# Two transformer blocks on one core: the first modulation weights in feature-block groups, and layer 1's first four projection pairs in plain fp32

## The reference, cut to what matters

```python
c_act = jax.nn.silu(c)                                # c: 1 x 1024
for l in range(2):
    mod = c_act @ w_ada[l] + b_ada[l]                 # w_ada[l]: 1024 x 6144
    sh1, sc1, gt1, sh2, sc2, gt2 = jnp.split(mod, 6, axis=-1)
    h = rms_norm(x, norm_mix[l]) * (1 + sc1) + sh1
    p = h @ w_in[l]                                   # 1024 x 7424
    qkv, p_rwkv, p_uv, gates = ...                    # columns of p
    # attention, an RWKV-7 time mix and a spatial gating unit on them, merged by the gates
    x = x + gt1 * (merged @ w_out[l])
    # the same with sh2, sc2, gt2 around a gated convolutional feed-forward net
```

## Time and profile before

| | us |
|---|---|
| median of 3 runs | 2301.24 (2300.49 to 2303.86) |
| the profiled execution, by the clock of the runs | 2303.23 |
| its span in the trace | 2301.4 |
| TensorE busy | 2245.0 (98%) |
| VectorE busy | 1646.5 (72%) |
| ScalarE busy | 1215.4 (53%) |
| mean granted TensorE clock | 0.986 of full |

### The profile page before, as it was taken

One profiled execution on the slowest core, in us unless ns is written; L12 is line 12 of the kernel. 1 busy time (PEld: TensorE's weight loads), 2 busy tenths in 40 slices (PEclk: granted clock), 3 DMA queues, 4 the chain that ended last, 5 costly groups with the idle time before them and its releaser, 6 DMA issues.

```text
span 2301.4 us, 42519 instructions
## 1 busy us (share of the span) xinstructions
PE 2245.0 (98%) x18142; PEld 2109.5 (92%) x18142; DVE 1646.5 (72%) x2455; ACT 1215.4 (53%) x1913; POOL 12.4 (1%) x20
## 2 busy tenths in 40 slices
PE   7999998999899999999999999999999999999999
PEld 7898988998888998999999898999899989899998
DVE  7777468987695649676666668776676666877666
ACT  3855345554655435455545457654555454675453
POOL 0000000000000000000000000000000000000000
PEclk8999999999999999999999999999999999999999
DMA  9444445776544345544555533455555553345553
GB/s 376 166 148 147 148 165 201 253 245 257 201 138 166 111 175 184 192 176 174 182 180 185 186 129 119 156 195 185 184 174 177 184 189 138 110 160 184 183 185 136
DMA packets 115293, 411.15 MB, mean 179 GB/s; under 512 B 12784, under 2 KB 15984, under 8 KB 114976
## 3 DMA queue, kind: packets, MB, share of 16 engines
q1 hardware_dynamic: 114816, 408.05, 50.4%
q10 hardware_dynamic: 288, 0.39, 0.0%
HBM read 407.32 MB, written 1.06 MB: 177 GB/s over the span
## 4 chain that ended last, share of the span: by engine, by line
PE 83%; DVE 10%; ACT 4%; issue 1%; DMA 1%; SPq 0%; POOL 0%; ACTq 0%; DVEq 0%
PE bank L196 83%; DVE lo L203 3%; DVE arena L211 2%; DVE arena L203 2%; ACT arena L240 2%; ACT L240 1%; ACT hi L240 1%; DVE xT L211 1%; PE bank L200 1%; DMA arena<-WA 1%; DVE acc L211 1%; DVE rs_t L217 0%; ACT h L240 0%; DVE h L211 0%; SPq L193 0%
## 5 line engine op out<-in xcount | busy, mean ns | idle before, releaser
L196 PE MATMUL bank<-h,hi 128*128 128x256 f32 (+1 forms) x6880 | 1275.4, 286 | 0.0
L196 PEld LDWEIGHTS bank<-h,hi 128*128 128x128 f32 x6880 | 1085.1, 193 | 10.0 <-issue 3.4
L240 ACT ACTIVATE hi<-raw 128x1024 fp32r<-128x1024 f32 x664 | 698.1, 1055 | 722.0 <-PE bank L196 683.3
L196 PE MATMUL bank<-h,lo 128*128 128x256 f32 x3504 | 1016.9, 290 | 20.7 <-DVE h L211 15.0
L203 DVE TENSOR_TENSOR lo<-raw,hi 128x1024 fp32r<-128x1024 f32 x664 | 804.1, 1220 | 96.9 <-ACT hi L240 96.0
L196 PEld LDWEIGHTS bank<-h,lo 128*128 128x128 f32 x3504 | 676.8, 193 | 35.8 <-DVE h L211 13.6
L196 PE MATMUL bank<-act,hi 128*128 128x512 f32 x1056 | 371.1, 393 | 0.0
L196 PE MATMUL bank<-act,lo 128*128 128x256 f32 x1056 | 298.8, 283 | 0.0
L196 PEld LDWEIGHTS bank<-act,hi 128*128 128x128 f32 x1056 | 198.4, 188 | 45.5
L196 PE MATMUL bank<-arena 64*64 64x64 f32 (+7 forms) x2994 | 223.4, 262 | 5.8 <-ACT arena L240 3.3
L196 PEld LDWEIGHTS bank<-arena 64*64 64x64 f32 (+3 forms) x2994 | 171.0, 146 | 37.9 <-issue 8.7
(11 more groups left out here) (143 smaller groups left out, 1882.7 us busy)
## 6 DMA issues: line engine op xcount, KB each, us to landing
raw<-W SPq DMA_DIRECT2D x664, 512.0 KB, 3.3
ada<-WA SPq DMA_DIRECT2D x80, 512.0 KB, 4.0
arena<-WA SPq DMA_DIRECT2D x16, 512.0 KB, 12.4
arena<-scr SPq DMA_DIRECT2D x2, 1024.0 KB, 9.6
xT<-x SPq DMA_DIRECT2D x1, 1024.0 KB, 7.7
arena<-lora SPq DMA_DIRECT2D x2, 512.0 KB, 9.2
arena<-wsT SPq DMA_DIRECT2D x2, 512.0 KB, 10.0
arena<-lnb SPq DMA_DIRECT2D x2, 512.0 KB, 10.3
```

The source lines that it names most:

```text
L196: return self.done(lambda e: e.matmul(out, l, r, start=start, stop=stop, skip_group_check=True))
L240: return self.done(lambda e: e.activation(out, in_, f, scale=scale, **kw))
```

## The change

1. The first 16 blocks of modulation weights hold the same numbers in another order: four groups of four blocks. Group p holds, for all eight k, the columns 2p, 2p + 1 (shift) and 8 + 2p, 9 + 2p (scale), so it completes the modulation of the feature blocks 2p and 2p + 1. They lie in the arena from its upper end down.
2. SP loads x and the first constants first, then group 0 and weight blocks 0 and 1, group 1 and blocks 2 and 3, group 2 and 4 and 5, group 3 and 6. The loads of lora, spatial weights and layer norm go behind group 1's accumulation, the remaining constants behind blocks 7 to 9, the next two modulation blocks behind block 10.
3. All four groups are accumulated by VectorE and summed by TensorE; `direct` is gone. After each group VectorE makes its bias sum, gain and two products, ScalarE the two shifted feature blocks in plain fp32 (`h whole`) and then their high parts; VectorE makes the low parts one group later.
4. The first four pairs of layer 1 (6, 2, 3, 0: 64 tiles, weight blocks 0 to 7) run with k as the outer loop, one plain fp32 matmul per tile on the unsplit weights (`start` in the tensor program). The sum of group 1, 2 and 3 stands on TensorE in the middle of feature block 1, 3 and 5. Blocks 0 to 7 are not split (`PLAIN`); the splits of blocks 8 to 12 lie in the start.
5. The four pairs take banks 0, 1, 4 and 5, the group sums banks 2, 6, 7 and 2; pair 1 takes bank 3.
6. The modulation chain is paused through the start, so its next unit begins after the RWKV chain's preparation, and it has 20 units after the start as before (one of the 21 chain units of before was begun at weight block 0, and the fourth group is new in the start). The RWKV chain starts after pair 0.

Layer 2 and the second stack keep their code.

```diff
+PLAIN = 8
...
-        self.n, self.at_block, self.sides, self.flags, self.mods = 0, at_block, {}, set(), set()
+        self.n, self.at_block, self.sides, self.flags = 0, at_block, {}, set()
+        self.mods = {(0, 0), (0, 1)}
...
+    n = FIRST * BT
     rest = [(l, m, 4) for l in range(L) for m in range(0 if l else FIRST, 48, 4)]
-    for i, (l, m0, w) in enumerate(rest, 3):
+    for i, (l, m0, w) in enumerate(rest, 4):
...
-        s += [("start1", l), ("z first", l)]
+        s += [("start1", l), ("z first", l)] if l else [("pause", True), ("start",)]
         for p in (6, 2, 3, 0, 1, 4, 5):
             s += [("z", l, p), ("flag", ("z", l, p))]
-            if p == 3:
+            if p == (3 if l else 0):
                 s += [("rwkv", l), ("pause", True)]
...
+Z_START, ADA_START = (0, 1, 4, 5), ((2,), (6,), (7,), (2,))
+Z_PAIRS = ((6, 2, 3, 0), (6, 2))
...
+            def start():                                      # TensorE
+                pairs = Z_PAIRS[0]
+                outs = [take(Z_START, ("z", 0, p)) for p in pairs]
+                start_sums(0)
+                for k in range(KD):
+                    for n, p in enumerate(pairs):
+                        if k % 2 and k < KD - 1 and n == 2:
+                            start_sums((k + 1) // 2)
+                        for j in range(2):
+                            w, ends = plain_tile(("w_in", 0, k, ("c", I_RWKV + (2 * p + j) * 128)))
+                            pe.wait_ge(a_main, ("h whole", k))
+                            i = pe.mm(t256(outs[n], j), w, t256(ht, k), k == 0 and j == 0, k == KD - 1)
...
+            def start_acc(p):                                 # VectorE
+                for k in range(KD):
+                    b, i = FIRST // 4 * p + k // 2, k % 2
+                    src = start_block(b)[:, i * 512:(i + 1) * 512]
+                    v.wait_ge(d_af[b], ("first ada", b))
...
+                        x = v.stt(ada_acc(p), src, cact[:, k:k + 1], ada_acc(p), MUL, ADD)
...
+            def start_x(p):
+                norm, two_k = ("n1", 0), slice(2 * p, 2 * p + 2)
+                v.wait_ge(pe_ad, ("sum", p))
...
+                for k in (2 * p, 2 * p + 1):
+                    v.stt(t256(ht, k), t256(xT, k), gsc[:, k:k + 1], rs_t, MUL, MUL).then_inc(v_main, ("hx", norm, k))
...
+            def start_low(p):
+                for k in (2 * p, 2 * p + 1):
+                    v.wait_ge(a_main, ("h", ("n1", 0), k))
+                    v.tt(t256(hl, k), t256(ht, k), t256(hh, k).bitcast(F32), SUB).then_inc(v_main, ("h", ("n1", 0), k))
...
+            def start():
+                start_acc(0)
+                factor(("n1", 0))
+                start_x(0)
+                v.ts(omu, P("rwkv_mu", 0, 0, 14), -1.0, 1.0, MUL, ADD).then_inc(v_main, ("omu", 0))
+                start_acc(1)
+                start_x(1)
+                start_low(0)
+                start_acc(2)
+                start_x(2)
+                start_low(1)
+                f.tiles(32)
+                start_acc(3)
+                start_x(3)
+                f.tiles(8)
+                start_low(2)
+                start_low(3)
+                f.tiles(24)
...
+            def start_x(p):                                   # ScalarE
...
+                    a.act(t256(ht, k), t256(ht, k), ACT.Identity, bias=shift1(0, k)).then_inc(a_main, ("h whole", k))
...
+                    a.act(t256(hh, k), t256(ht, k), ACT.Copy).then_inc(a_main, ("h", norm, k))
...
+                elif what == "start":
+                    deviation(("n1", 0))
+                    for p in range(3):
+                        start_x(p)
+                    f.tiles(32)
+                    start_x(3)
+                    f.tiles(32)
...
+            s.dma(xT[:, :], T["x"]).then_inc(d_x, "x")        # SP
+            s.dma(cst[:, ident:cos], T["cst"][:, ident:cos]).then_inc(d_cst0, "cst0")
+            for p in range(4):
+                load_start(p)
+                for b in (2 * p, 2 * p + 1) if p < 3 else (6,):
+                    load(b)
...
+                elif what == "start":
+                    f.tiles(16)
+                    s.wait_ge(v_ad, ("acc", 1, 7))
+                    load_small(0)
+                    f.tiles(8)
+                    s.dma(cst[:, cos:NCST], T["cst"][:, cos:NCST]).then_inc(d_cst, "cst")
...
+                    f.tiles(8)
+                    for b in range(FIRST, FIRST + RAWA):
+                        load_ada(b)
+                    f.tiles(32)
```

More of the change, by code:

```diff
@@ L641, in ada @@
                 use = ("ada", l, g)
[L642 to L654, removed]
+                if what == "sum":
+                    if j0 == 0:
                         take(ONE, use)
@@ L675, in tile, with start_sums, plain_tile @@
                 return hi[b % HL][:, cols], lo[b % RAW][:, cols], [("block", b)] if i + n == BT else []
+            def start_sums(p):
+                o = take(ADA_START[p], ("ada start", p))
+                pe.wait_ge(d_cst0, "cst0")
+                pe.wait_ge(v_ad, ("acc", p, 7))
+                for j in range(4):
+                    x = pe.mm(o[:, 2 * j:2 * j + 1], ada_acc(p)[:, j * 128:(j + 1) * 128], C("one"), True, True)
+                x.then_inc(pe_ad, ("sum", p))
+            def plain_tile(key):
+                b, i = divmod(f.n, BT)
+                if e is None:
+                    order.append(key)
+                pe.wait_ge(d_raw[b % RAW], ("raw", b))
+                f.n += 1
+                return raw[b % RAW][:, i * 128:(i + 1) * 128], [("block", b)] if i == BT - 1 else []
+            def start():
[10 more added lines that the diff above has]
+                            i = pe.mm(t256(outs[n], j), w, t256(ht, k), k == 0 and j == 0, k == KD - 1)
+                            names = ends + ([("z", 0, p)] if k == KD - 1 and j == 1 else [])
+                            if names:
+                                i.then_inc(pe_main, *names)
+                            if ends:
+                                f.tick()
             def h_in(norm):
@@ L1070, in tensor_program @@
                     f.need(*q)
+                elif what == "start":
+                    squares(("n1", 0), range(8))
+                    start()
                 elif what == "start1":
                     l = q[0]
-                    if l == 0:
-                        squares(("n1", 0), range(8))
                     f.need(l, 0)
                     f.need(l, 1)
-                    if l:
-                        squares(("n1", 1), ["sum", 6, 7])
+                    squares(("n1", l), ["sum", 6, 7])
                     f.slow = False
@@ L1281, in normed @@
+            def normed(norm, l, shift):
                 v.wait_ge(v_main, ("rs", norm))
@@ L1292, in normed @@
                         v_main, ("h", norm, k))
-                    if k in splits:
-                        split(splits[k])
             def gain(norm, l, at, name):
@@ L1956, in deviation, with normed @@
                 a.act(var_t, statb[:, 0:256], ACT.Sqrt, bias=C("eps6")).then_inc(a_main, ("sd", norm), frees=("stat", norm))
-            def normed(norm, l, shift, splits=()):
+            def start_x(p):
+                norm = ("n1", 0)
+                a.wait_ge(v_ad, ("mod start", p))
+                for k in (2 * p, 2 * p + 1):
+                    a.wait_ge(v_main, ("hx", norm, k))
+                    a.act(t256(ht, k), t256(ht, k), ACT.Identity, bias=shift1(0, k)).then_inc(a_main, ("h whole", k))
+                for k in (2 * p, 2 * p + 1):
+                    a.wait_ge(a_main, ("h whole", k))
+                    a.act(t256(hh, k), t256(ht, k), ACT.Copy).then_inc(a_main, ("h", norm, k))
+            def normed(norm, l, shift):
                 for k in range(8):
@@ L2481, in pool_program @@
                     f.need(*q)
+                elif what == "start":
+                    f.tiles(64)
                 elif what == "start1":
```

148 lines of the change are left out of this document (62 added, 86 removed).

## The result

The changed kernel took 2305.1 us (median of 20 runs, 2302.33 to 2307.66), the kernel before 2301.54 (20 runs, 2299.62 to 2303.97): ratio 1.0014, 95% interval 1.0007 to 1.0020. The forecast was 2297.1, the range 2291.5 to 2303.0. The profiled execution took 2307.51 us, its span 2305.7.

The account below looks back on a forecast made before the run. TensorE, busy 98% of the span, bounds the kernel, so only its waits or work taken off it pay, mostly at the start. −7.5 + 2.4 + 1.0 = −4.1 us from 2301.24 gave 2297.1, range 2291.5 to 2303.

Parts of the forecast that it names:

- Part 1: Kernel start up to the first projection: root ends last at 15.4 us, first projection at 18.5 us against 35.48.
- T0: Mark at the start of the first projection matmul: forecast 18.5 us, before 35.48.
- Part 2: First projection to end of the first four pairs: VectorE paces sums 9.3 us apart, end at 54.8, gain 6.7 us.
- T1: Mark at the end of the first four pairs (64 weight tiles): forecast 54.8 us, before 61.46.
- Rival (c): Slower: TensorE at 1.2 GHz through the start, T1 = 79, kernel 2321 us; chance 10%.
- Part 3: End of the first four pairs to end of block 26: net −0.3, gain 7.0 us, 7.5 with a later wait partly gone.
- T2: Mark at the end of block 26 (first qk block): before 135.98 us, forecast 128 to 130.
- rival (a): VectorE's full stretch takes the gain back: 5 us of TensorE waits instead of 1.5, kernel 2300.6 us; chance 16%.
- Part 4: After block 26: layer 1 nothing, layer 2's out projection +2.4 us, a modulation sum in its up projections +1.0.
- the late accumulations: Four modulation accumulations forecast to fall into layer 2's out projection, on a chain of VectorE alone: +2.4 us.

Follow-up runs that it names:

- e6: Changed kernel with layer 1's keys step one block later and one idle step behind it taken out: 2308.72 us, 1.0027 of the kernel before.
- g11: e7 with one idle step of layer 1's RWKV chain, behind its length step, left out: 2297.35 us, 0.9980 of the kernel before.
- g9: Changed kernel with the fill alone (modulation chain at full rate from pair 14 of layer 1's up projection): 2302.22 us, 1.0002 of the kernel before.
- e7: e3 plus the fill of g9: 2298.53 us, 0.9984 of the kernel before.
- e3: Changed kernel with the bank counter advanced by two at the first pair of the second stack's first mixer: 2302.26 us, 0.9999 of the kernel before.
- e1: Changed kernel with the bank counter advanced by two at layer 1's second norm: 2303.77 us, 1.0003 of the kernel before.
- e8: Changed kernel with the low parts of blocks 10, 12, ... 24 computed by GpSimd instead of VectorE: 2312.35 us, 1.0043 of the kernel before.

## Why the prediction was wrong

**Part 1, right in its number, a little lucky in its cause.** T0 18.34 us against 18.5. The root was to end last, at 15.4, a microsecond behind the accumulations. They ended together, the root at 14.93 and the accumulations at 15.11, and VectorE went from one to the other without idling:

```profile
14.46 0.47 ACT L241 ACTIVATE var_t<-bank,cst 128x256 f32<-128x256 f32 x1
```

```profile
9.43 5.68 DVE L212 SCALAR_TENSOR_TENSOR arena<-arena,sml 128x512 f32<-128x512 f32 x7
15.02 1.75 DVE L218 RECIPROCAL rs_t<-var_t 128x256 f32<-128x256 f32 x1
```

**Part 2, right, two sizes off against each other.** T1 54.97 against 54.8, the gain 6.5 against 6.7. The first 12 tiles took 6.9 us and not 8.1, as some 3 us of it ran at half clock and not 6; the sums' spacing was 9.1 to 9.2 for 9.3, paced by VectorE as said; the last 20 tiles took 10.57 for 8.6, at a clock that fell there instead. The bytes came at 419 GB/s and no block's weights were waited for after sum 1. Rival (c) did not happen, though its sign, half clock past 27 us, did for 3.4 us.

**Part 3, the first step that failed.** "Net −0.3: gain at T2 = 7.0", with 0.5 more for the wait ahead of the inverse. It was 3.8 instead of 7.5. The step took the RWKV chain as held at its time and 1.5 us of waits, with the 0.16 that stood there some 1.7 in all; in fact TensorE, 6.5 us ahead, met the chain at three places (0.37, 2.25 and 1.51 us, 4.1 in all against 2.1 before). And it had no term for the clock: TensorE ran at half clock behind the 2.25, where seven tiles took 4.1 us (99.54 to 103.65) instead of 7 × 0.36 = 2.5: 1.6. So 2.4 of waits and 1.6 of clock cover the 3.7 that are missing. This is rival (a), given 16%, which put 3.5 us there, and its sign, over 3 us of waits, came true; but the rival named VectorE's load as the cause, and the runs speak for the chain in series. VectorE and ScalarE each wait for the other in that stretch, and TensorE's lead was used up against the chain's length. That the chain's length does it is argued from e6 and g11; no run shortened the chain and gained clear of the scatter.

**Part 4, right but for one size.** Layer 2's out projection +2.4 forecast, 2.5 measured; the sum +1.0 forecast, 0.5 measured; nothing in layer 1.

**What the prediction did not have.** The bank rotation: +2.9 − 0.8 = 2.1 us, and the clock that falls behind the wait. Part 3 did count the banks of the four pairs and where each was wanted again, but not that `take` advances one counter for the whole program, so that five turns fewer at the start move every bank from there on. And the clock: outside stage A the changed kernel spent some 50 us at 1.2 GHz (20 runs, span times twice the part of the clock withheld, less 10.2 for A), the kernel before 46 (33 runs, less 20.5), and 44 in the last set: 5 to 7 us more, which at 0.4 is 2 to 2.7 us (a line through the times of single runs mostly has only 0.2 to 0.35 us per microsecond, 1 to 2 in all).

The sum by the runs: A −3.8, D +2.5, E +0.5, the rotation +2.1, together +1.3; the clock 1 to 2.7; measured +3.6, by its interval 1.6 to 4.6. The sum closes within that. Of the clock's part about 1 lies in stage F behind the new wait. The rest goes largely with the late accumulations: g9 against the changed kernel and e7 against e3 differ only by the fill, and have 6 to 8 us less at half clock, while e1, which only puts the banks right, keeps its 61.9. Why the stretches at half clock come and go between executions of one kernel stays open.

## What to carry to other kernels

A resource that is dealt out by a counter (banks, buffers, semaphores) couples places that have nothing else in common: when an edit changes how often it is turned, compare the allocation behind the edit too, and look for the one place where two uses in a row fall on the same one, above all where a second list deals out some of the same banks. A lead won for one engine can be worth no more than the serial chain beside it leaves, so before counting it, follow that chain to the next place where they meet. And spare vector work belongs where TensorE bounds without a wait, not where the vector engine only looks idle because it is waiting.

## What the runs showed of the hardware

GpSimd stopped VectorE outright (e8). While GpSimd ran two subtractions of 128x1024, four scans took 5.73 us on VectorE, against 1.35 in the kernel after; later a scaling of 128x4 elements took 2.31 instead of 0.16 and ended with GpSimd's subtraction (101.46 and 101.43):

```profile
83.70 5.14 POOL L205 TENSOR_TENSOR lo<-raw,hi 128x1024 fp32r<-128x1024 f32 x2 [9.22 <-ACT hi L242]
...
98.93 2.50 POOL L205 TENSOR_TENSOR lo<-raw,hi 128x1024 fp32r<-128x1024 f32 x1 [10.09 <-ACT hi L242]
```

```profile
84.02 5.73 DVE L225 TENSOR_TENSOR_SCAN arena<-cst,arena 128x128 f32<-128x128 f32 x4
...
99.15 2.31 DVE L209 TENSOR_SCALAR sml<-par 128x4 f32<-128x4 f32 x1
```

These two places cost 4.4 and 2.2 us; they delayed the chain, and TensorE waited 8.09 us at gmlp's bank at 105.54. A third followed at 109.50, where VectorE's own subtraction took 3.42 us instead of 1.22. Of the 9 us taken off VectorE, 8.7 were paid back in these three places. The Trainium skill, page "SBUF — State Buffer", section "Who interferes with whom", says that the two engines share a pair of ports that one of them holds for a whole instruction while the other is blocked. The trace agrees, with 2.31 us against 0.16.
